# Differential heads: the two maps' hi-query times lo-key products as two 64-row tiles of the TensorE array

## The reference, cut to what matters

```
def diff_attend(q, k, v, lam):
    s = jnp.einsum('bhjqd,bhjnd->bhjqn', q, k) * (HEAD_DIM ** -0.5)
    p = jax.nn.softmax(s.astype(jnp.float32), axis=-1)
    a = (p[:, :, 0] - lam * p[:, :, 1]).astype(v.dtype)
    return jnp.einsum('bhqn,bhnv->bhqv', a, v)
```

## Time and profile before

| | |
|---|---|
| timed runs | 2087.32 us median |
| span of the profiled execution | 2084.2 us |
| PE busy | 1818.6 us (87%), 9456 matmuls |
| DVE busy | 1218.3 us (58%) |
| ACT busy | 828.5 us (40%) |
| POOL busy | 630.4 us (30%) |
| scores matmuls, lines 834 and 835 | 288 each, parts 0 to 2 |
| chain that ended last | PE 67%, DVE 16%, issue 9%, ACT 5%, DMA 2% |

### The profile page before, as it was taken

The page is one execution under the profiler, slowest core; times in us unless marked ns, Lnnn a source line. Parts: engine busy times, 40 slices in busy tenths (PEclk is TensorE's granted clock), DMA queues, the critical chain, the costliest instruction groups (busy, mean ns, idle before and its releaser), DMA issues.

```text
span 2084.2 us, 26369 instructions
## 1 busy us (share of the span) xinstructions
PE 1818.6 (87%) x9456; PEld 1556.0 (75%) x9456; DVE 1218.3 (58%) x2125; ACT 828.5 (40%) x1452; POOL 630.4 (30%) x324
## 2 busy tenths in 40 slices
PE   5877987786896998999999978799886889999997
PEld 1776777674685887888888868778775668888886
DVE  2765757656558688755415665576566466335255
ACT  3345664545423333133213334465555334334242
POOL 1123532212111333422322322252322124444442
PEclk9988999896897999999999989799996889999999
DMA  8210013000142223333324331100100123232332
GB/s 327 85 45 8 1 57 106 20 21 1 61 152 71 99 95 139 123 130 121 101 81 130 122 117 54 38 1 16 51 21 21 51 71 101 93 99 91 101 100 82
DMA packets 45166, 166.94 MB, mean 80 GB/s; under 512 B 4752, under 2 KB 4752, under 8 KB 43920
## 3 DMA queue, kind: packets, MB, share of 16 engines
q1 hardware_dynamic: 41696, 156.25, 22.2%
q10 hardware_dynamic: 3376, 9.44, 1.2%
HBM read 161.48 MB, written 4.19 MB: 79 GB/s over the span
## 4 chain that ended last, share of the span: by engine, by line
PE 67%; DVE 16%; issue 9%; ACT 5%; DMA 2%; DVEq 0%; SPq 0%; POOL 0%; ACTq 0%
PE ps L736 19%; PE ps L737 18%; PE ps L738 18%; DVE nb L1636 2%; PE ps L834 2%; DVE ada_junk L1339 2%; PE ps L835 2%; PE ps L755 2%; PE ps L845 2%; DVE pt_lo L1613 1%; PE ps L933 1%; PE ps L720 1%; ACT qk L1085 1%; DMA w_raw<-w_d 1%; DVE p_sb L1605 1%
## 5 line engine op out<-in xcount | busy, mean ns | idle before, releaser
L667 POOL TENSOR_TENSOR w_lo<-w_raw,w_hi 128x1024 fp32r<-128x1024 f32 (+1 forms) x200 | 474.1, 2374 | 1195.0 <-ACT w_hi L1007 1195.0
L736 PE MATMUL ps<-h_hi,w_hi 128*128 128x512 f32 (+1 forms) x1056 | 376.2, 356 | 5.9 <-DVE h_lo L1427 5.9
L737 PE MATMUL ps<-h_lo,w_hi 128*128 128x512 f32 (+1 forms) x1056 | 376.0, 356 | 0.0
L738 PE MATMUL ps<-h_hi,w_lo 128*128 128x512 f32 (+1 forms) x1056 | 375.2, 355 | 0.0
L1007 ACT ACTIVATE w_hi<-w_raw 128x1024 fp32r<-128x1024 f32 (+1 forms) x200 | 201.3, 1007 | 360.5 <-PE ps L738 236.5
L736 PEld LDWEIGHTS ps<-h_hi,w_hi 128*128 128x128 f32 x1056 | 201.0, 190 | 34.8 <-issue 6.4
L698 POOL TENSOR_TENSOR p_sb<-p_sb,ri 128x768 f32<-128x768 f32 (+1 forms) x120 | 156.1, 1307 | 233.3 <-DVE p_sb L1605 126.6
L737 PEld LDWEIGHTS ps<-h_lo,w_hi 128*128 128x128 f32 x1056 | 201.1, 190 | 28.0
L738 PEld LDWEIGHTS ps<-h_hi,w_lo 128*128 128x128 f32 x1056 | 200.8, 190 | 28.1
L736 PE MATMUL ps<-w_hi,h_hi 128*128 128x384 f32 (+1 forms) x560 | 191.0, 341 | 17.2 <-DVE h_lo L1427 12.4
L1636 DVE TENSOR_REDUCE nb<-ps 128x1 f32<-128x768 f32 (+1 forms) x160 | 135.1, 847 | 111.7 <-PE ps L835 111.4
(11 more groups left out here) (133 smaller groups left out, 3315.4 us busy)
## 6 DMA issues: line engine op xcount, KB each, us to landing
w_raw<-w_d SPq DMA_DIRECT2D x152, 512.0 KB, 3.5
ada_b<-ada_d SPq DMA_DIRECT2D x64, 512.0 KB, 3.6
w_raw<-w_d SPq DMA_DIRECT2D x48, 384.0 KB, 3.1
ada_first<-first_d SPq DMA_DIRECT2D x4, 2048.0 KB, 19.7
ada_first<-ada_d SPq DMA_DIRECT2D x4, 1024.0 KB, 11.5
x_sb<-x_d SPq DMA_DIRECT2D x1, 3072.0 KB, 12.1
x_sb<-x_d ACTq DMA_DIRECT2D x1, 3072.0 KB, 10.3
c_bc<-cc_d SPq DMA_DIRECT2D x2, 1024.0 KB, 8.8
```

Of the source, the lines that this page charges most:

```text
L667: nc.gpsimd.tensor_tensor(w_lo[:, c % RING, 0:n], w_raw[:, c % RAW, 0:n], w_hi[:, c % RING, 0:n].bitcast(f32), ALU.subtract).then_inc(w_lo ...
L736: nc.tensor.matmul(out, lh, rh, start=first, stop=False)
L737: nc.tensor.matmul(out, lh, rl_, start=False, stop=False)
L738: return nc.tensor.matmul(out, ll, rh, start=False, stop=last)
```

## The change

In parts 1 and 2, PE now issues both maps of a query tile at the list position of map 0, and nothing at that of map 1. For each map it first issues the [q; q] with [k_hi; k_hi] matmuls over all 128 rows. Then, piece by piece, it issues q_hi with k_lo alone, over 64 rows: map 0 on partitions 0 to 63, map 1 on partitions 64 to 127, into their two different PSUM tiles. The product q_lo with k_lo is no longer computed for these heads. So that map 1's q_hi lies in partitions 64 to 127, `tile_hi` and `tile_lo` now write the two query maps with one instruction each, the second with its halves exchanged. DVE's and ACT's lists, the PSUM banks and all other waits stay as they are.

```diff
-                    if kind == "S":
-                        sid, m = s["sid"], s["m"]
-                        if p == 0:
-                            qs, ks = it["h"], 8 + 2 * (it["h"] // (A_HEADS // A_KV))
-                        else:
-                            qs, ks = 2 * it["h"] + m, 4 + 2 * (2 * it["h"] + m)
+                    if kind == "S" and p == 0:
+                        sid = s["sid"]
+                        qs, ks = it["h"], 8 + 2 * (it["h"] // (A_HEADS // A_KV))
...
+                    elif kind == "S":
+                        if s["m"]:
+                            continue
+                        sid = s["sid"]
+                        tok = slice(s["q"] * P, (s["q"] + 1) * P)
+                        pieces = [(k, min(k + 512, it["k1"])) for k in range(it["k0"], it["k1"], 512)]
+
+                        def bank(m, k0, k1):
+                            return ps[:, 2 * ((sid + m) % 2) + (k0 - it["k0"]) // 512, 0:k1 - k0]
+
+                        for m in range(2):
+                            qs = 2 * it["h"] + m
+                            if sid + m >= 2:
+                                pe.wait_ge(exp_done, sid + m - 1)
+                            for k0, k1 in pieces:
+                                nc.tensor.matmul(bank(m, k0, k1), qk[:, qs, tok], qk[:, 4 + 2 * qs, k0:k1],
+                                                 start=True, stop=False)
+                        for k0, k1 in pieces:
+                            for m in range(2):
+                                qs, half = 2 * it["h"] + m, slice(HD * m, HD * m + HD)
+                                mm = nc.tensor.matmul(bank(m, k0, k1), qk[half, qs, tok], qk[half, 5 + 2 * qs, k0:k1],
+                                                      start=False, stop=True)
+                                if k1 == it["k1"]:
+                                    mm.then_inc(scores_done, 1)
...
-                        ins = A(split[:, i, b:b + n, 0, :].bitcast(f32r), u, ACT.Copy, scale=SCALE)
+                        if ch["p"] == 0:
+                            ins = A(split[:, i, b:b + n, 0, :].bitcast(f32r), u, ACT.Copy, scale=SCALE)
+                        else:
+                            for m in range(n):
+                                ins = A(split[:, i, b + m, m, :].bitcast(f32r), roped[:, i, s0 + m, :], ACT.Copy,
+                                        scale=SCALE)
...
-                        ins = V.scalar_tensor_tensor(split[:, i, b:b + m, 1, :], u, SCALE, split[:, i, b:b + m, 0, :],
-                                                     ALU.mult, ALU.subtract)
+                        if ch["p"] == 0:
+                            ins = V.scalar_tensor_tensor(split[:, i, b:b + m, 1, :], u, SCALE,
+                                                         split[:, i, b:b + m, 0, :], ALU.mult, ALU.subtract)
+                        else:
+                            for j in range(m):
+                                ins = V.scalar_tensor_tensor(split[:, i, b + j, 1 - j, :], roped[:, i, s0 + j, :], SCALE,
+                                                             split[:, i, b + j, j, :], ALU.mult, ALU.subtract)
```

## The result

The changed kernel takes 2162.69 us (median, 2159.83 to 2170.22) against 2086.34 (2080.83 to 2087.75; four runs, one more than the forecast had): 1.0385 times the kernel before, 95% interval 1.0367 to 1.0403. That is +76.4 us where +72.4 were forecast. The profiled execution spans 2158.3 us, 74.1 more than the one before.

A forecast was written before the change was run, and what follows sets the result against it. Bank-pair loops, not PE, were taken to bound the fronts, and pairing merges two into one. Fronts, T0 to T2, 256 keys and splits gave 74.4, less 2: +72.4 on 2087.3, 2160 us, range 2130 to 2180.

The forecast's parts named there:

- What bounds: Fronts of differential parts (S0 to T0): the loop of scores, maximum, exponential over PSUM banks bounds, despite PE 87% busy.
- The low-clock cycle: Fronts of part 1 at the low clock: two loops become one, 6.35 us per pair against 3.72.
- The lo block's middle value: A pair's two 64-row lo products: 0.96 us, between 0.64 with full overlap and 1.28 with none.
- The fronts: S0 to T0 of four differential parts: +16.4 and +18.6 us in the parts 1, +12 in each part 2.
- T0 to T2: Item 0 of each differential part: 3.31 us becomes one cycle, 6.35 or 5.5; net 2.05, four times, +8.2 us.
- 256 keys: Layer 0's 256-key maps: 1.64 us a pair becomes 2.9; two cycles in each of two parts, +5.2 us.
- Splits and starting clock: Extra query split instructions on 40 tiles, +2 us; first two pairs of layer 1 part 1 at high clock, -2.
- The signs named ahead: Fronts of part 1: odd maxima 6.3 us apart, DVE waiting some 2 us before even maxima, lower PE share.
- The clock did not stay high in the fronts: Rival: clock high in four fronts, cycles 0.85 us shorter, +48, 2135 us; chance 0.20 together with cover in part 2.
- The tiles do overlap: Rival: 64-row tiles don't overlap, 0.32 us more on eight pairs of four parts, +10, 2170 us; chance 0.15.
- DVE did not cover part 2: Rival: DVE's work covers the loop in part 2's fronts, +48, 2135 us; chance 0.20 together with high clock.
- PE does not set the pace: Rival: array time bounds these stretches, so pairing gives back some 15 us, 2072 us; chance 0.03.

The follow-up runs named there:

- pair_full_rows: Changed kernel with both maps still issued together, but lo products over all 128 rows and the old query splits; 2162.93 us, 1.0369 to the kernel before.
- wide_front: Changed kernel with a second set of four PSUM banks for six pairs in each front of part 1; 2134.27 us, 1.0248 to the kernel before.
- splits_only: Kernel before with only the changed kernel's query splits (`tile_hi`, `tile_lo`); 2081.61 us, 0.9986 to the kernel before.
- pair_same_rows: Changed kernel with old splits and both maps' 64-row lo products in the same half of the array; 2179.67 us, 1.0441 to the kernel before.
- tiles_unpaired: Kernel before, each map at its own place, with 64-row lo products and the new query splits; 2145.77 us, 1.0304 to the kernel before.
- wide_pairs_only: The candidate: changed kernel pairing only six pairs per part 1 front, with second banks; other maps single over all rows; 2091.48 us, 1.0036 to the kernel before.

## Why the prediction was right

*What bounds.* Right. That a pair's loop, not PE, sets the fronts was read from one cycle of the timeline, and `pair_full_rows` and `wide_front` show it from both sides.

*The low-clock cycle.* 6.35 forecast, 6.32 measured. By its terms: hi, lo and hand-off 0.80 + 0.96 + 0.24 = 2.00, measured 402.29 to 404.27 = 1.98; map 0's maximum with `finish` 2.31, measured 2.30; maximum and exponential 2.04, measured 400.26 to 402.29 = 2.03. The lo block's middle value of 0.96 met 0.94. Hi to lo took 0.94 instead of 0.80: the sum had put nothing there for the first change of the array's division. The hand-off was 0.10 instead of 0.24. That these two cancel is luck.

*The fronts.* Forecast +16.4, +12, +18.6, +12, sum 59.0. Measured +15.3, +12.7, +17.0, +13.2, sum 58.1. In layer 0 part 1 the 1.2 us too many are in the first pair: from S0 to map 1's hi products of the second pair it took 4.43 us (378.90 to 383.33), not 5.5. It began at a granted clock of 1.00 (378.90 to 380.41), so that map 0's maximum started 1.51 us after S0 and not 2.64. Five cycles of 6.32 follow. In part 2 the period of two steps was forecast at 9.65 us. It is 9.69 between the even maxima below, in the timeline of DVE, and 9.70 between PE's hi products of map 1 (515.53 to 525.23):

```profile
517.52 0.96 DVE L1667 TENSOR_REDUCE nb<-ps 128x1 f32<-128x768 f32 x1 [2.95 <-PE ps L855]
...
527.21 0.96 DVE L1667 TENSOR_REDUCE nb<-ps 128x1 f32<-128x768 f32 x1 [3.61 <-PE ps L855]
```

DVE's own work did not cover the loop: it waited 2.95 and 3.61 us for PE.

*T0 to T2.* 3.31, 3.61, 3.90 and 3.43 us before, 5.61, 6.32, 5.73 and 5.54 after: +8.9, forecast +8.2.

*256 keys.* This term was too small, 5.2 forecast. Windows over the whole attention show it. Those of part 1 in layer 0 and in layer 1, before:

```profile
378.18:436.87 58.69, 44.50 (x184) 33.80 (x185) 42.06 (x88) 31.38 (x69) 16.00 (x13) 0.79 0.03 10
...
1493.45:1537.79 44.34, 30.01 (x149) 22.24 (x149) 33.80 (x60) 23.35 (x46) 13.55 (x9) 1.00 0.04 13
...
```

And after:

```profile
378.90:459.62 80.72, 50.01 (x184) 32.29 (x185) 42.10 (x88) 30.96 (x69) 15.99 (x13) 0.66 0.02 7
...
1533.22:1596.19 62.97, 37.98 (x148) 23.75 (x149) 33.97 (x60) 23.51 (x46) 13.54 (x9) 0.70 0.03 9
...
```

These two grow by 22.0 and 18.6 us, the parts 2 by 20.8 (70.33 to 91.15) and 14.8 (57.62 to 72.39), all together 76.2. Less the fronts (58.1) and T0 to T2 (8.9), 9.2 are left. By part that is 4.5 and 5.4 in layer 0, which has the 256-key maps, and -0.2 and -0.5 in layer 1, which has none. The step had priced their cycle at the high clock, 2.9 us. The clock in that stretch is 0.68 where it was 1.00, and the even maxima are 3.44 us apart, in the timeline of DVE:

```profile
436.74 0.42 DVE L1667 TENSOR_REDUCE nb<-ps 128x1 f32<-128x256 f32 x1 [1.34 <-PE ps L855]
...
440.18 0.42 DVE L1667 TENSOR_REDUCE nb<-ps 128x1 f32<-128x256 f32 x1 [1.71 <-PE ps L855]
```

In `pair_full_rows` the same stretch had a granted clock of 1.00, and there even maxima are 2.85 us apart (440.74 to 443.59): the 2.9 of the sum. On those maps the tiles lose at the low clock, 0.21 us of columns saved against 0.44 for the division. From map 1's hi product to the end of the lo block it is 1.02 us (439.06 to 440.08), and over all rows, in `pair_full_rows`, 0.81 (446.20 to 447.01). The sum also counted two periods where there are three: between the even maxima of S16, S18, S20 and S22 lie 2.56, 3.44 and 4.23 us in part 1 (434.18 to 444.41), before 1.62, 1.64 and 2.56 (416.34 to 422.16), 4.4 more. In part 2 it is 4.1 more, and 1.3 of its 5.4 stay open.

*Splits and starting clock.* The splits were forecast at +2 and cost nothing that can be told (`splits_only`). The -2 for the first two pairs of layer 1 part 1 is inside the measured front. In sum 58.1 + 8.9 + 9.2 = 76.2, against the forecast's 59.0 - 2 + 8.2 + 5.2 + 2 = 72.4; outside these parts 2 us went the other way. That the total is off by only 1.7 us of span is in part luck: the three terms above came out 5.8 us higher than the forecast's, and the splits with the rest of the program 4.1 lower.

*The signs named ahead.* Even maxima wait for PE, odd ones don't: seen. The wait is 2.99 us and not "some 2": the forecast's own cycle leaves nearly that, since 6.35 less 2.31 and less the second maximum's 0.88 is 3.2. Map 1's first matmul is released by `ptmp`, and PE's share is lower: seen.

*The rivals.* The clock did not stay high in the fronts (0.53, 0.50, 0.57, 0.50). The tiles do overlap. DVE did not cover part 2. PE does not set the pace: `pair_full_rows`, with all the columns of before, is no slower than the changed kernel beyond the noise (1.0369 and 1.0385). Array time does count in the loop that the pairing made, since `pair_same_rows`, with a cycle 0.43 us longer, is at 1.0441; but that is small beside the 2.60 us that a pair lost.

## What to carry to other kernels

Before array time is taken away, look at which loop the stretch turns in. Two maps that alternate over two bank pairs are two loops side by side, and an edit that issues both at one place makes them one, so that everything on the reading engines between the two reads comes onto the path (here 2.60 us a pair). Where a pair shares its banks with the next, put the previous pair's leftovers ahead of the wait (40 us here); where its banks are doubled, leave them where they are. Doubled banks undo the merging but brought no gain: with them the kernel before was 0.1% slower and the candidate 0.4%. Count each change of the array's division as a fixed price against the columns it saves.

## What the runs showed of the hardware

- A change between all 128 rows and 64-row tiles costs 0.30 us at the low clock, whether 512 or 256 columns follow (`tiles_unpaired`: 0.73 for 0.43, 0.51 for 0.21). In a pair it shows as 0.14 ahead of the lo block and 0.30 in it. At the high clock the lo block is 0.56 us (changed kernel, 1684.62 to 1685.18), where one map's 768 columns take 0.36: 0.20. Where array work follows directly, 0.16 more falls on that: after the last pair of `wide_pairs_only` a 512-column matmul starts its successor after 0.59 us (401.00 to 401.59), not 0.43. A matmul that follows a wait takes 0.59 anyway, so there the third share is not felt.
- Two 64-row matmuls in different halves of the array run fully side by side: 0.94 us against 1.58 in the same half, with 0.30 of a change in each.
- Together, with 768 keys at the low clock, a pair saves 0.64 us and pays 0.44 where the array waits afterwards, and 0.60 where it goes on: with 256 keys it saves 0.21 and loses (1.02 us against 0.81).
- A PE without gaps by its rows need not be at the high clock: in the front of `tiles_unpaired` (378.99 to 409.71) it is busy 30.51 of 30.72 us, at a granted clock of 0.54.
